# Down projections of a two-layer diffusion backbone as seven half products instead of eight

## The reference

```python
h = h + g1 * y                                   # y: the mixer's output product
h = h + g2 * swiglu(modulate(rmsnorm(h, norm2_g[l]), sh2, sc2), ffn_w_gu[l], ffn_w_down[l])

def swiglu(h, w_gu, w_down):                     # w_gu: 1024 x 5632, w_down: 2816 x 1024
    gt, up = jnp.split(h @ w_gu, 2, axis=-1)
    return (jax.nn.silu(gt) * up) @ w_down

def short_conv_mixer(h, w_in, w_conv, w_out):
    bg, cg, xv = jnp.split(h @ w_in, 3, axis=-1)
    return (bg * dwconv(cg * xv, w_conv, SC_PAD)) @ w_out
```

## Time and profile before

| what | value |
|---|---|
| median of the runs | 2292.92 us (2291.8 to 2294.6) |
| profiled execution: span, first to last instruction | 2288.6 us |
| PE busy | 2234.8 us, 98% of the span, 10246 matmuls |
| DVE, POOL, ACT busy | 65%, 50%, 37% |
| chain that ended last | PE 85%, DVE 6% |
| granted TensorE clock, mean | 0.995 of full speed |

### The profile page before, as it was taken

The page is one execution under the profiler, slowest core; times in us unless marked ns, Lnnn a source line. Parts: engine busy times, 40 slices in busy tenths (PEclk is TensorE's granted clock), DMA queues, the critical chain, the costliest instruction groups (busy, mean ns, idle before and its releaser), DMA issues.

```text
span 2288.6 us, 27308 instructions
## 1 busy us (share of the span) xinstructions
PE 2234.8 (98%) x10246; PEld 1822.6 (80%) x10246; DVE 1484.0 (65%) x1897; ACT 840.3 (37%) x1396; POOL 1143.8 (50%) x726
## 2 busy tenths in 40 slices
PE   8999999999899999999999999999899999999998
PEld 3788887878688888888888778888688888888886
DVE  5677856854876555558777987665965555555553
ACT  4555546853523332331213522233533333332212
POOL 3323304788455555565434345574365555564340
PEclk9999999999999999999999999999999999999999
DMA  9756568734132222257662122260132222242321
GB/s 332 223 159 175 159 177 205 163 131 134 42 101 83 83 83 83 83 192 258 207 208 78 51 74 74 74 215 2 60 102 90 83 83 83 84 151 90 111 83 74
DMA packets 296942, 282.95 MB, mean 124 GB/s; under 512 B 64783, under 2 KB 242155, under 8 KB 296299
## 3 DMA queue, kind: packets, MB, share of 16 engines
q1 hardware_dynamic: 258747, 257.61, 36.4%
q10 hardware_dynamic: 37488, 21.50, 3.3%
q0 software_dynamic: 576, 2.10, 0.2%
HBM read 226.36 MB, written 57.16 MB: 124 GB/s over the span
## 4 chain that ended last, share of the span: by engine, by line
PE 85%; DVE 6%; DMA 2%; ACT 2%; issue 2%; POOL 1%; SPq 0%; ACTq 0%; DVEq 0%; POOLq 0%
PE bank L1102 27%; PE bank L1104 26%; PE bank L1103 26%; PE bank L1191 1%; DMA q_spill<-qk_raw 1%; PE bank L1332 1%; DVE act_lo L2138 1%; DVE act_hi L2138 1%; PE bank L1357 1%; PE bank L1145 1%; PE bank L1316 1%; PE bank L1358 0%; DVE probs L2519 0%; DVE x_rms L2130 0%; DMA k_lo<-k_spill 0%
## 5 line engine op out<-in xcount | busy, mean ns | idle before, releaser
L2057 DVE SCALAR_TENSOR_TENSOR h<-bank,mods,h 128x512 f32<-128x512 f32 x384 | 287.4, 750 | 260.4 <-PE bank L1104 255.3
L1063 POOL TENSOR_TENSOR slot_lo<-pair_raw,slot_hi 128x512 fp32r<-128x512 f32 x112 | 169.8, 1516 | 288.0 <-ACT slot_hi L1621 288.0
L1063 POOL TENSOR_TENSOR slot_lo<-t_sum,slot_hi 128x512 fp32r<-128x512 f32 x109 | 164.5, 1531 | 153.4 <-ACT slot_hi L1621 153.4
L1063 POOL TENSOR_TENSOR slot<-pair_raw,slot 128x512 fp32r<-128x512 f32 x144 | 232.2, 1634 | 16.0 <-ACT slot L1621 16.0
L2218 DVE TENSOR_TENSOR bank<-bank,p 128x512 f32<-128x512 f32 x53 | 37.0, 698 | 288.3 <-PE bank L1104 288.2
L1102 PE MATMUL bank<-act_lo,slot_hi 128*128 128x512 f32 x436 | 171.1, 392 | 6.6 <-DVE act_lo L2138 5.9
L1621 ACT CAST slot_hi<-pair_raw 128x512 fp32r<-128x512 f32 x112 | 69.0, 616 | 294.4 <-DMA pair_raw<-in_ffn_w_gu 243.6
L1102 PE MATMUL bank<-a,slot_hi 128*128 128x512 f32 x436 | 171.5, 393 | 2.8 <-ACT p L1630 0.9
L1104 PE MATMUL bank<-a,slot_hi 128*128 128x512 f32 x436 | 170.5, 391 | 0.0
L1103 PE MATMUL bank<-act_lo,slot_lo 128*128 128x512 f32 x436 | 169.9, 390 | 0.0
L1104 PE MATMUL bank<-act_lo,slot_hi 128*128 128x512 f32 x436 | 169.9, 390 | 0.0
(11 more groups left out here) (329 smaller groups left out, 5975.0 us busy)
## 6 DMA issues: line engine op xcount, KB each, us to landing
pair_raw<-in_ffn_w_gu SPq DMA_DIRECT2D x88, 512.0 KB, 4.6
mod_in_f<-in_mod_w SPq DMA_DIRECT2D x48, 512.0 KB, 3.7
z_spill<-silu_g SPq DMA_DIRECT2D x88, 256.0 KB, 2.6
mod_in_p<-in_mod_w SPq DMA_DIRECT2D x32, 512.0 KB, 4.5
pair_raw<-in_o_w_in SPq DMA_DIRECT2D x24, 512.0 KB, 3.8
raw<-in_e_w_in SPq DMA_DIRECT2D x20, 512.0 KB, 4.4
low_f<-z_spill SPq DMA_DIRECT2D x40, 256.0 KB, 5.1
a_f<-z_spill SPq DMA_DIRECT2D x18, 512.0 KB, 6.2
```

The source lines that it names most:

```text
L1063: nc.gpsimd.tensor_tensor(low, from_, high, ALU.subtract).then_inc(s_wlo, 1)
L2057: V.scalar_tensor_tensor(out=dst, in0=bank[:, b, :], scalar=mods[:, gate, m:m + 1], in1=dst, op0=ALU.mult, op1=ALU.add).then_inc(s_hup, 1)
```

## The change

For z and the down weight the change takes two 128-row tiles as the two halves of the inner axis (a **kp**: 11 in F, 4 in S), features 0 to 511 and 512 to 1023 as the two halves of the outputs, and the token halves, and makes seven half products where the block form has eight.

- `DOWN` lists the seven products q: weight block or weight sum, z block or z sum, and the four PSUM banks (`XS` or `YS`) they add up in. A product q runs over all kp as **steps** of 12 matmuls (`down_part`; 77 steps in F, 28 in S). `UPDATES` says to which quarters of h the banks are added after q; there are 36 updates of 128 x 512 per stage (before, 160, in S 48).
- **Sums of z** (`z_sum`): four subtractions of 128 x 512 per kp on DVE, placed in `before_pair` (ahead of a pair's sums) and after the last product of z. Seven blocks per kp are stored in `z_parts` instead of four.
- **Sums of weights** (`w_sum`): four per kp on POOL, from pair 4 of a stage on at three per pair, between the low halves. `load_w` brings the four blocks of 256 KB per kp, `store_w` puts the four sums in `w_sums` (DRAM). They live in the space of h.
- So **h is in DRAM** meanwhile: `put_h_aside` stores its 4 MB in pair 1, `bring_h_back` loads it in the last pair but one (in S in the last one).
- **Modulation pieces** (`mod_unit`): two per pair, 32 in F0 from pair 4 on, 16 in S from pair 3 on, summed in SBUF in place of PSUM.
- **Loads of the down phase** (`load_step`): two of 256 KB per step into a ring of eight; one low half of each step by POOL, the other by DVE from step 4 on.
- The norm of the next stage's first token half moves to products q = 3 to 5. The **last rows**: rows 0 to 3 during q = 5, of rows 4 to 7 the upper features during q = 6 and the lower ones after it; ACT scales the upper halves.

The core of the diff:

```diff
+        DOWN = (((0, 0), B11, XS, True), (S2, T2, YS, True), ((1, 0), B21, XS, False), (S3, T3, YS, False),
+                ((1, 1), T4, YS, False), (S1, T1, XS, True), (S4, B22, XS, False))
+        UPDATES = (((0, 1), (1, 0), (1, 1)), ((0, 1),), ((0, 0),), ((1, 1),), ((1, 0),), ((1, 1),), ((0, 1),))
...
+            def aside_work(st, p):
+
+                for k in w_ops(st, p):
+                    store_w(st, k)
+                for r in w_loads(st, p):
+                    load_w(st, r)
+                for u in mod_units(st, p + 1):
+                    load_mod_f(u)
+                if p == (PAIRS[st] - 2 if st != S else PAIRS[st] - 1):
+                    bring_h_back(st)
...
+                    z_from = pair_kind(st, p - 1)[0] != "sum"
+                    if z_from:
+                        store_b(st, p - 1, 0)
+                    if p > 1 and p + 1 < PAIRS[st]:
+                        load_pair(st, p + 1, 1)
+                    if z_from:
+                        store_b(st, p - 1, 1)
+                    if p > 1 and p + 1 < PAIRS[st]:
+                        load_pair(st, p + 1, 0)
+                    if p == 1:
+                        put_h_aside(st)
...
+                    if st != S and p % 2:
+                        store_t(KP0[st] + p // 2, T1)
+                    if st != S and p % 2 == 0:
+                        for c in (T3, T2, T4):
+                            store_t(KP0[st] + p // 2 - 1, c)
+                    aside_work(st, p)
...
                 for p in range(1, PAIRS[st]):
+                    sums = w_ops(st, p - 1)
                     for n in operands(st, p):
                         operand_low(st, n, p)
-                for r in range(ROUND[st]):
-                    down_low(st, r)
+                        if n in (1, 3, 5) and len(sums) > n // 2:
+                            w_sum(st, sums[n // 2])
+                down_lows(st)
...
+                mm = product(bank[:, banks[m], :], (w[0][:, at_], w[1][:, at_]), x[0], x[1], fresh and r == 0, end, not fresh)
...
+                if c == T1:
+                    dve.wait_ge(*stored(B11, kp + 1))
+                    ins = V.tensor_tensor(a, b, a, ALU.subtract)
...
+                else:
+                    dve.wait_ge(*stored(B21, kp + 1))
+                    dve.wait_ge(*z_summed(kp, T2))
+                    ins = V.tensor_tensor(c_, c_, t2, ALU.subtract)
...
+                if st != S and p % 2:
+                    dve.wait_ge(s_z1, PAIR0[st] + p)
+                    z_sum(KP0[st] + p // 2, T1)
+                if st != S and p % 2 == 0 and p:
+                    for c in (T2, T4):
+                        z_sum(KP0[st] + p // 2 - 1, c)
+                for u in mod_units(st, p):
+                    mod_unit(u)
```

More of the change, by code:

```diff
@@ new lines, in feature, with step_done, down_operand @@
+        def feature(n, i):
+            return (i + 4) % FT if n in (N_S + 1, N_F1 + 1) else i
+        def step_done(st, i):
+            q, r = divmod(i, KP[st])
+            if r == KP[st] - 1:
+                return out_done(st, q, 3)
+            return s_step, sum(6 * (KP[k] - 1) + KP[k] - TAIL for k in range(st)) + q * (KP[st] - 1) + r + 1
+        def down_operand(i):
+            s = i % RING
+            if s < 4:
+                return tuple((act_lo[:, k, one], act_lo[:, k, two], low_f[:, k, two]) for k in (2 * s, 2 * s + 1))
+            if s < 6:
+                return tuple((act_hi[:, k, two], act_hi[:, k + 1, two], x_rms[:, k + 1, two]) for k in (4 * s - 16, 4 * s - 14))
+            return tuple((a22[:, k, one], a22[:, k, two], a22_f[:, k, two]) for k in (2 * s - 12, 2 * s - 11))
@@ new lines, in down_landed, with down_high_at, down_low_at @@
+        def down_landed(st, i):
+            before = sum((steps_of(k) - i % RING + RING - 1) // RING for k in range(st))
+            return s_land[i % RING], MOD_DONE + 32 * (before + i // RING + 1)
+        def down_high_at(st, i, j):
+            return s_h2, 2 * sum(steps_of(k) for k in range(st)) + 2 * i + j + 1
+        def down_low_at(st, i, j):
+            if j == 1 and i >= BOTH:
+                return s_lz, sum(steps_of(k) - BOTH for k in range(st)) + i - BOTH + 1
+            return s_l2, sum(steps_of(k) + BOTH for k in range(st)) + (2 * i + j + 1 if i < BOTH else i + BOTH + 1)
@@ L1636, in silu_first @@
-                if p:
-                    act.wait_ge(s_zst[0], 16 * done)
-                nc.scalar.activation(silu_g[:, 0, :], bank[:, x_bank(p), :] if p else silu_g[:, 0, :], ACT.Silu).then_inc(s_xfree, 1)
+                if kp and p % 2 == 0:
+                    act.wait_ge(*stored(T1, kp))
+                    act.wait_ge(*z_summed(kp - 1, T2))
+                if kp and p % 2:
+                    act.wait_ge(*stored(T4, kp))
+                to = zt[:, p % 2, one]
+                nc.scalar.activation(to, bank[:, x_bank(p), :] if p else to, ACT.Silu).then_inc(s_xfree, 1)
@@ L1653, in first_tap @@
+                act.wait_ge(*z_summed(kp - 1, T4))
                 c = PAR["short_w"] + tile
[L1654 to L1661 removed]
@@ L1724, in pair_work @@
                 for n in range(7):
+                    if ahead is None and n == 3:
+                        down_high(st, 0)
+                        down_high(st, 1)
+                    if ahead is None and n == 6:
+                        down_high(st, 2)
+                        down_high(st, 3)
                     if n == 3 and st != S:
@@ L2306, in mods_here @@
-            def mods_here(r, idx):
-                for u in mod_units(r, idx):
+                        steps.run(V.scalar_tensor_tensor(out=zt[:, tile % 2, :], in0=t_pad[:, j:j + SEQ], scalar=par[:, c:c + 1],
+                                                         in1=zt[:, tile % 2, :], op0=ALU.mult, op1=ALU.add))
+                else:
+                    V.tensor_tensor(zt[:, 0, two], first, zt[:, 0, two], ALU.mult).then_inc(s_z0, 1)
+                    V.tensor_tensor(zt[:, 1, two], c22, zt[:, 1, two], ALU.mult).then_inc(s_z1, 1)
```

922 lines of the change are left out of this document (536 added, 386 removed).

## The result

The changed kernel takes 2526.64 us (median of four runs, 2520.1 to 2530.57) against 2292.51 of the kernel before in the same session: a ratio of 1.1017, 95% interval 1.0999 to 1.1036. The forecast was 2442 with a range of 2340 to 2525: slower, as forecast, but by 234 us instead of 150, and 1.6 us above the range. The profiled execution has a span of 2528.6 us, 240.0 more than before; it was the longest of the four (2530.57 us). The time of a run is 1.8 to 2.0 us longer than its span, in this run and all later ones. So of the 4.3 us that were put on the forecast's span some 2.3 belong to a profile of before that was quicker than the median, not to what lies around the first and the last instruction.

What follows compares the result with a forecast made beforehand. PE's matmuls were taken to bound the kernel, PE being busy 98%. On the 2288.6 us span, -70.8 + 70 + 30 + 126 + 2 - 5 - 2 = +150 gave about 2438; with 4.3 for the median, 2442, range 2340 to 2525.

Steps and rivals of the forecast that it cites:

- two circles: Pair phases: loops of waits through POOL, SP and transfers, said to make rounds longer than PE's 19.1 us per pair.
- all hidden: Down steps: work of POOL, ACT, DVE, SP and the queue said to fit beside PE's 2.72 us per step.
- S's pairs: Pair phase of S: a round of 21.4 + 4.5 us, with fewer stores of z, costing +30 us.
- the lead over PE: Pairs: low halves finished before PE needs them, 6.8 us for the first, 5.7 for the second, subtracted from lost time.
- PE's gain: Down phases of F and S: 312 fewer matmuls at 0.2268 us each, -70.8 us, all on PE's path.
- The first circle: Pairs: POOL's seventh low half, raw weight reload, ACT's cast, POOL's next low half; 21.4 us with sums, F1 24.2, +70.
- The second circle: F0's pairs: DVE's z sum waits for a z store issued after POOL's third sum; round 27.9 us, +126 us.
- by the rows' worst duration: Pairs: DVE and POOL sharing SBUF ports said to cost at most 0.5 us per operation.
- The third rival: More contention: slower POOL operations add 2 us to 35 rounds, modulation steps slow likewise, or down steps collide; 2525 us, 10%.
- The first, no burden by the queue: Rival for the pairs: transfers overlap and only SP's issuing counts, 0.38 us each; about 2350 us, 22%.
- The second, that the sums hide: Rival for the pairs: rounds stay below 19.55 us with all added work, so PE never waits; 2215 us, 5%.
- the room lies inside the reload: Pairs: only 2.24 + 0.45 of POOL's idle 8 us are outside the reload, so a sum must take under 0.9 us.

Runs made afterwards that it cites:

- third_late_mods: Changed kernel with third weight sum stored after the next pair's z stores and raw loads, modulation loads ahead of the sums' stores: 2346.6 us, ratio 1.0235.
- z_first: Changed kernel with SP storing the first half of z before the store of the pair's third weight sum: 2509.2 us, ratio 1.0949.
- in_gap: Changed kernel with POOL's three sums after the seventh low half, stored after the raw loads, their weight loads one pair later: 2271.8 us, ratio 0.9912.

## Where the prediction was right, and where it failed

The measured 2526.64 us lies outside the stated range and 84.6 us above the forecast of 2442. Slower, and by two circles through POOL and SP, came as forecast, and the rounds in F are nearly as priced. What failed are terms of the sum. The first is S's down phase: its steps were taken as "all hidden", -9 us, and it measured +17.3. Part of that is shown to be the order of ACT's program, which the forecast did not look at (below); the rest stays open. The second is S's pairs, +30 forecast and +53.4 measured. The third is the lead over PE that was taken off in each stage, 19 us in all, which was not there.

**PE's gain.** F0's downs with the join took 38.9 us less (forecast 35), the end 29.1 (32). Seven products at 2.72 us a step, full clock, h's transfers hidden: right in F.

**The first circle.** Right in size. Bare of SP's waits it is 21.7 and 21.05 us in the two F stages (third_late_mods), forecast 21.4. With raw loads behind the third sum F1 has 24.75, forecast 24.2.

**The second circle.** Right in F0 in place and nearly in size: 28.5, forecast 27.9. That F1's would be well hidden, at 23, was not right: from 1900 to 2180 us DVE waits 82.8 us for stores of z and PE 27.9 us for DVE's second sum. Yet with z stored first (z_first) F1's round falls by 0.3 us only, so the two circles are nearly equal there. And the modulation loads are a gate of it on their own, which the forecast counted only as time in the queue.

**Where 90 us were missed.** The table's second and third lines give it by term, on the spans of the profiled executions (on the medians it is 84.6).

- *The lead that was taken off*, 5.7 in F0, 6.8 in S and in F1: 19.3 us. The forecast let PE live on finished operands at first. But PE waits for DVE's second sum of the very same pair, and DVE has no lead: the first round with a store of sums behind it, the one after pair 4, took 30.9 us at once.
- *The rounds*, 0.6 us too short in each F: 9.5 in F0 and 8 in F1. The rest of F0's miss is 4.6, and 2 of F1's.
- *S's pairs*, +53.4 for +30, of which 6.8 are the lead. The forecast priced S by the first circle with fewer stores of z. Its round came to 25.9 us; the mean of the rounds from pair 4 to 9 is 28.8. A gate there that the forecast did not have is DVE's wait for the modulation loads, 25.9 us from 1440 to 1600, beside 12.7 for stores of z. Moved ahead, these loads gave 14 us of S, the z store 3; as moving them also spares the raw blocks the time in the queue that the forecast did count, the share of the gate alone stays open.
- *S's downs*, +17.3 for -9: 26 us, the largest single term, and the step that failed outright. "All hidden" was judged by each engine's work in a step, not by its order: ACT's cast of F1's first weights stood in front of the casts for the down steps and waited 10.9 us for its load, and PE then waited 8.7 us. With F1's casts and low halves six steps later both waits are gone, and 9.3 us came back. In S's 28 steps the updates, the squares of F1's norm and the low halves of the next stage also fall together, and DVE's operations took 1.75 us instead of 0.69, 1.06 more each, where the forecast allowed at most 0.5 per operation "by the rows' worst duration". Its own rows 7 have 0.69 to 1.80 for the DVE form, 1.1 apart; 0.5 is POOL's difference. What that cost, and the other 17 us, was not taken apart: the cause of these stays open.
- *Small ones*: 4.6 before F0, 2.8 at the end, less 4.0 at F0's downs.

19.3 + 9.5 + 4.6 + 8 + 2 + 16.6 + 26.3 + 4.6 + 2.8 - 4.0 makes 89.7, the 90 of the spans but for rounding. The third rival (more contention, 2525, 10%) had the right time largely by luck: it put 2 us more on each round, which the rounds in F do not show, and a collision in the down steps, which only S's had.

**The rivals.** The first, no burden by the queue, falls by the run with light loads (83 us less with an eighth of the columns). The second, that the sums hide, is wrong for this order of work, yet it describes in_gap: POOL's idle time is enough for three sums if nothing waits behind them. The forecast's argument against it, that the room lies inside the reload, was an argument about the place of the sums and not about the change's idea.

The clock was left out of the forecast. PE's windows show it below full wherever PE waits, 0.86 in F0's pairs. There 1020 matmuls held PE for 252.8 us where the pitch from the earlier trace rows asks for 231; but a round set by the circles holds that loss in its idle time, and no run here prices it alone.

## What to carry to other kernels

Before moving work to an engine with idle time, ask what that idle time is waiting for and what will now stand behind the new work in every in-order queue: the same sums cost 110 us between the halves and next to nothing in the reload, but only after SP's stores of them were put behind the loads that the next round needs. A blocked store at the head of an issuing queue delays all that is issued after it; when one late transfer is moved ahead, look at once for the next one behind the same wait. And check the short stages by themselves, in the order of each engine's program: 28 steps of S lost what was "hidden" in F's 77, in part because ACT was given work for the next stage whose load had not landed.

## What was not expected of the hardware

DVE and POOL took turns. With POOL's subtractions of two SBUF tensors running without a gap, DVE's operations on two SBUF tensors took 1.75 us against 0.69 alone and POOL's 1.71 against 1.29, each engine starting one every 1.67 us. The Trainium skill, "SBUF — State Buffer", section "SBUF: two separate sides", says that whichever of such a pair starts first holds the shared ports for the whole instruction while the other fully blocks, and that PE, ACT and DVE's own pair of ports wait for nobody. The rows agree in the main: the addition at 1770.84 that reads one of its operands from a bank takes 0.70 us while POOL's operation at 1770.37 is under way. But one operation of each in 1.67 us is less than the 0.69 + 1.29 = 1.98 us of the two alone, so a part of them still overlapped. How much of S's loss this made, no run here shows.
